# Start addresses in SBUF: weights, xT and the arena on multiples of 2048 bytes, and half the scratch of the software DMA queue

## What is computed

```python
y = (gated_branches(x @ w_in)) @ w_out
x = x + gx1 * y
x = x + gx2 * (square(relu(h @ w_mlp1)) @ w_mlp2)
```

## Time and profile before

| what | value |
|---|---|
| median of 3 runs | 2089.11 us (2085.4 to 2089.83) |
| span of the profiled execution | 2089.1 us, from its first to its last instruction |
| instructions | 36236 |
| TensorE, matmuls | 2024.6 us busy |
| TensorE, weight loads (beside the matmuls) | 1789.9 us busy |
| VectorE | 1363.7 us |
| ScalarE | 1019.1 us |
| GpSimd | 162.3 us |
| granted TensorE clock, mean | 0.991 of full |
| read from HBM | 291.93 MB, 140 GB/s over the span |

### The profile page before, as it was taken

One profiled execution on the slowest core, in us unless ns is written; L12 is line 12 of the kernel. 1 busy time (PEld: TensorE's weight loads), 2 busy tenths in 40 slices (PEclk: granted clock), 3 DMA queues, 4 the chain that ended last, 5 costly groups with the idle time before them and its releaser, 6 DMA issues.

```text
span 2089.1 us, 36236 instructions
## 1 busy us (share of the span) xinstructions
PE 2024.6 (97%) x13946; PEld 1789.9 (86%) x13946; DVE 1363.7 (65%) x2114; ACT 1019.1 (49%) x2014; POOL 162.3 (8%) x174
## 2 busy tenths in 40 slices
PE   6999999999999999999999999999999999999998
PEld 5899657888788888879967999999998989888897
DVE  5699688344565564577977667776766555886455
ACT  5475575324422322358457454445824444675443
POOL 0000000000000001000000002223120111000110
PEclk9999999999999999999999999999999999999999
DMA  7322374222222222233255545554302555443553
GB/s 287 122 82 102 122 283 161 81 101 101 81 83 98 100 100 83 98 108 135 83 203 217 179 147 181 185 192 176 115 21 82 181 181 188 184 164 137 191 183 121
DMA packets 40896, 294.56 MB, mean 141 GB/s; under 512 B 4544, under 2 KB 4544, under 8 KB 5456
## 3 DMA queue, kind: packets, MB, share of 16 engines
q1 hardware_dynamic: 40464, 290.73, 38.4%
q0 software_dynamic: 320, 2.26, 0.3%
HBM read 291.93 MB, written 1.05 MB: 140 GB/s over the span
## 4 chain that ended last, share of the span: by engine, by line
PE 88%; DVE 5%; ACT 4%; issue 1%; DMA 1%; SPq 0%; DVEq 0%; ACTq 0%
PE psum L652 21%; PE psum L654 21%; PE psum L653 20%; PE psum L1017 3%; PE psum L1021 3%; PE psum L1018 3%; PE psum L890 2%; PE psum L1224 2%; DVE weights_lo L1964 2%; PE psum L793 2%; PE psum L912 1%; PE psum L692 1%; PE psum L693 1%; PE psum L694 1%; ACT weights_hi L1363 1%
## 5 line engine op out<-in xcount | busy, mean ns | idle before, releaser
L1964 DVE TENSOR_TENSOR weights_lo<-raw_weights,weights_hi 128x2048 fp32r<-128x2048 f32 x225 | 512.6, 2291 | 163.1 <-ACT weights_hi L1363 162.7
L1363 ACT ACTIVATE weights_hi<-raw_weights 128x2048 fp32r<-128x2048 f32 x225 | 429.0, 1910 | 152.6 <-DMA raw_weights<-in_weights 133.1
L2043 DVE SCALAR_TENSOR_TENSOR xT<-psum,mods,xT 128x256 f32<-128x256 f32 x408 | 181.0, 479 | 199.9 <-PE psum L654 196.5
L652 PE MATMUL psum<-h_hi,weights_hi 128*128 128x512 f32 (+1 forms) x832 | 279.9, 336 | 0.1
L654 PE MATMUL psum<-h_lo,weights_hi 128*128 128x512 f32 (+1 forms) x832 | 279.8, 336 | 0.0
L653 PE MATMUL psum<-h_hi,weights_lo 128*128 128x512 f32 (+1 forms) x832 | 278.1, 334 | 0.0
L2840 POOL TENSOR_TENSOR ffsq<-ff 128x256 f32<-128x256 f32 (+1 forms) x128 | 118.2, 925 | 1592.1 <-ACT ff L1450 1107.6
L652 PE MATMUL psum<-weights_hi,h_hi 128*128 128x256 f32 x704 | 197.5, 280 | 0.0
L653 PE MATMUL psum<-weights_lo,h_hi 128*128 128x256 f32 x704 | 195.5, 278 | 0.0
L654 PE MATMUL psum<-weights_hi,h_lo 128*128 128x256 f32 x704 | 195.5, 278 | 0.0
L652 PE MATMUL psum<-g_hi,weights_hi 128*128 128x256 f32 x688 | 193.7, 282 | 0.0
(11 more groups left out here) (423 smaller groups left out, 4277.6 us busy)
## 6 DMA issues: line engine op xcount, KB each, us to landing
raw_weights<-in_weights SPq DMA_DIRECT2D x273, 1024.0 KB, 4.8
staged_x<-in_x_rows SPq DMA_DIRECT2D x1, 2048.0 KB, 10.0
masks<-in_masks POOLq DMA_DIRECT2D x1, 1152.0 KB, 6.8
ln_rows<-in_ln_rows POOLq DMA_DIRECT2D x1, 1024.0 KB, 6.8
out<-outrow SPq DMA_DIRECT2D x4, 256.0 KB, 2.1
rows<-in_rows SPq DMA_DIRECT2D x1, 584.0 KB, 9.7
consts<-in_consts SPq DMA_DIRECT2D x1, 388.0 KB, 3.8
cols<-in_cols SPq DMA_DIRECT2D x1, 306.0 KB, 2.8
```

The source lines that it names most:

```text
L652: mm(out, *pair(wh, vh), start=i == 0, stop=False)
L1363: f(w_hi[:, s, :], raw[:, s, :], ACT.Copy).then_inc(hi_done, 1)
L1964: tt_(w_lo[:, s, :], raw[:, s, :], w_hi[:, s, :].bitcast(F32), ALU.subtract).then_inc(lo_done, 1)
L2043: last = stt(xT[:, m, c], b[:, c], mods[:, l, which + m, v:v + 1], xT[:, m, c], ALU.mult, ALU.add)
```

## The change

Four edits of constants. The ring of raw weights is moved to address 10240 with a filler tile below it; weights_hi and xT follow it directly and so lie at 43008 and 75776. The arena is rounded up to a multiple of 4096 instead of 64 and lies at 110592. The software queue's scratch is 8192 bytes instead of 16384. The order of the tiles, the offsets within the arena and all instructions are as before. The small tables between xT and the arena move with the ring.

```diff
-        ring_at = -(-nc.sbuf_base // 64) * 64
+        sb("below_ring", [P, (10240 - -(-nc.sbuf_base // 64) * 64) // 4])
+        ring_at = 10240
+        assert nc.sbuf_base == ring_at
         raw = sb("raw_weights", [P, RAW, CHUNK])
...
         ARENA = 112 * 1024
-        arena_at = -(-nc.sbuf_base // 64) * 64
+        arena_at = -(-nc.sbuf_base // 4096) * 4096
...
-    nc = bacc.Bacc("TRN2", target_bir_lowering=False, num_devices=1)
+    nc = bacc.Bacc("TRN2", target_bir_lowering=False, num_devices=1, dynamic_dma_scratch_size=8192)
```

## The result

The changed kernel takes 2096.1 us (median of 6 runs, 2092.97 to 2101.57) against 2088.74 for the kernel before: ratio 1.0037, 95% interval 1.0022 to 1.0052. It is slower, by 7.4 us. (One of the six executions of the kernel before took 5204.07 us; without it their median is 2088.38 and the difference 7.7.) The profiled execution of after spans 2099.8 us, 10.7 more than that of before, and was the longest of its six.

What follows compares the result with a forecast made beforehand. TensorE was taken as the bound (97% busy, 88% of the chain matmuls). From 2089.1 us, TensorE's reads, the splits and the scratch counted 0 and DMA -0.3, giving 2088.8 us; range 2060 to 2104.

Steps and rivals of the forecast that it cites:

- no effect: Likeliest case for the whole kernel: 2088.8 us, own range 2084 to 2093, chance 0.43.
- the case on the slower side: Rival: streamed and loaded operands on equal phase collide, TensorE's level rises; 2109 us in full, 2099 half, chance 0.25.
- TensorE's reads: Term for operand start addresses in matmul triples: taken as 0, between +20 and -24 us.
- that of the rise: Sign of TensorE slowing: pitch over 0.2288 at 700 us or over 0.118 at 150 us.
- that of the fall: Sign of TensorE speeding up (chance 0.32): 0.1133 at 1300 us, or 512 columns under 0.2288 at 700.
- the sign of a wrong reason: Product stretches 550 to 880 and 1250 to 1410 us changing length by over 1 us at equal matmul count.
- The phase modulo 2048 beyond the phase modulo 1024 is worth nothing: Streamed rows at TensorE: crossing a 2048-byte line costs nothing, from even 0.34 us steps and xc_hi's equal booked time.
- An address can't tell those two apart; what came before them can: 256-column stretches at 110 and 150 us: same addresses, different level, so the TensorE term was taken as 0.
- The bounds: Limits on the TensorE term, priced by the trace's two pitch levels: +20 us upward, -24 us downward.
- ScalarE and VectorE, 0: Weight splits (copy 1910 ns, subtraction 2291 ns, 225 times each) unchanged: 0; 1% on both would be 1.9 us.
- DMA, -0.3 us: First transfers' waits at the start, 19.4 us: 3% gain or loss allowed, 0.6 us, half taken.
- The scratch, 0: Halved software-queue scratch for GpSimd's three transfers: cost 0 because covered; 7 us without cover.

Runs made afterwards that it cites:

- x1: Kernel before with only the scratch halved, every tile 8192 bytes lower (ring 8320, arena 106432): 2089.63 us, ratio 1.0002.
- y3: Changed kernel with the arena at 110656, ring still at 10240, restoring the old distances 64 and 192: 2090.94 us, ratio 1.0014.
- x4: Changed kernel with ring (10304) and arena (110656) both 64 bytes past a multiple of 2048, distance 0: 2095.91 us, ratio 1.0042.
- x3: Changed kernel with the ring at 8320, its old phase, and the arena kept at 110592, distance 128: 2112.34 us, ratio 1.0111.
- x2: Changed kernel with the arena at 110528, its old phase, and the ring kept at 10240: 2091.46 us, ratio 1.0010.
- v2: y3 with g, the second network's ff, and h, o and ff of the first network's 256-token layer 128 bytes lower: 2072.14 us, ratio 0.9916.
- z1: x2 with h_hi and h_lo 128 bytes lower: 2090.07 us, ratio 1.0001.
- z2: z1 with ff also at distance 0 for the 512-token MLP and the second network: 2090.25 us, ratio 1.0006.
- v3: v2 with h and ff of the first network's 512-token MLP also at distance 0: 2068.92 us, ratio 0.9896.

## Why the prediction was wrong

The measured 2096.1 us lies inside the range, 2060 to 2104, but the likeliest case was no effect (0.43), and the effect is clear: the case on the slower side, given 0.25, came true in sign, with 7.4 us of its 20. The term that failed is TensorE's reads, put at 0; the product stretches grew by 11.8 us. The signs that were to tell the cases apart came mixed: 0.1200 at 150 us is that of the rise, 0.2266 between 620 and 860 us that of the fall. By these pitches the 1536 matmuls of the first long stretch take some 3 us less and the 1536 of the second some 3 us more, both over the 1 us that was named as the sign of a wrong reason. That the time lies between two of its cases is luck: two effects of opposite sign left a small rest.

- **What bounds the kernel**: right. All of the change lies in TensorE's pitch, none in waits.
- **"The phase modulo 2048 beyond the phase modulo 1024 is worth nothing"**: right, and too weak a test. Steps of 1024 bytes are multiples of 256, so they could not show a period of 256. At 200 us the steps are even in before, x1, y3, after and x4, but not at every distance: in x3 they run from 351 to 362 ns.
- **"An address can't tell those two apart; what came before them can"** is the step that failed. From two levels at one address I took it that addresses set nothing, and the term became 0. The table shows that d sets which pitches are possible. At the distances of the kernel before, 192 and 64, 113.4 and 117.8 ns both are; at d = 0 neither is, and all stretches of over 40 matmuls of 256 columns took 119.6 to 120.0. At 512 columns each d has its pitch to within 1 ns. "Nearest row" was a comparison within one d, which says nothing of another d.
- **The bounds** of +20 and -24 us held, though made of the wrong parts. I bounded each kind by the two levels in the trace; 256 columns went above both (0.1200 against 0.1180) and 512 columns below both (0.2266 against 0.2288). The term for 512 columns had the wrong sign in the rival that came true: it expected +9.7 us from the arena and got -5.4, and the 256-column terms gave +23.5 in place of 9.9.
- **The rival's mechanism**, equal phases that delay each other's reads, fits the 256-column matmuls (x4 shows that equal phases alone bring them) and is contradicted by those of 512, which are at their best with equal phases. A name like "collide" was worth no more than its price.
- **ScalarE and VectorE, 0**: right, 2291 and 1909 ns. **DMA, -0.3 us**: not resolved; the weights land in 4.8 us at either start, so the extra transaction of the Trainium skill, "DMA: Bandwidth & Descriptors", section "How a descriptor splits into AXI transactions", doesn't show in a 1 MB transfer's landing. **The scratch, 0**: right, shown by x1.
- The Trainium skill, "SBUF — State Buffer", section "Who interferes with whom", gives TensorE two read ports, one for the streamed operand and one for the weight load, and calls them independent. The runs differ from that: the pitch moves by up to 3% at 512 columns and 6% at 256 with nothing but the distance of the two operands. That no other engine delays TensorE, which the prediction takes from there, is not tested as such, but the effect needs none: with nothing else at work the pitches move all the same, 229.1 to 226.7 and 117.3 to 120.0 ns.

Open: whether the distance that counts is to the block loaded for the same matmul or to the one being loaded for the next, since in every stretch all loaded blocks had the same d; and what decides between the levels of 256 columns, at d = 192 above all.

## What to carry to other kernels

When TensorE is bound by back-to-back float32r matmuls, measure the pitch of starts by shape and by operand order, and try the distance of the operands' start addresses modulo 256 in steps of 32 or 64 bytes before believing in round addresses; here the distance is worth from -1.0% to over +1%, at no instruction. Compare executions at the same granted clock: here some 5 us of difference came from it. A layout that is best for one matmul shape can be worst for another, so choose it by tile and by stage. Tiles whose stretches alternate did best at one place modulo 256 (second window: x2 and v2 against z1 and z2), though v3 shows that this alone does not hold the lower level. Where the same work shows two speeds at one address, that tells that history matters, not that the address doesn't.

## What was not expected of the hardware

- The pitch of a 256-column matmul with its weight load ranges from 0.1132 to 0.1200 us, that of 512 columns from 0.2266 to 0.2344, as a function of the distance of the two operands' starts modulo 256 bytes, not monotonically: 226.8, 233.2, 228.9, 233.5, 232.4, 234.3, 233.3, 233.3 ns for 512 columns in steps of 32 bytes.
- At distances 192 and 64 a 256-column matmul has two stable pitches, 0.1133 and 0.1178 us. A stretch keeps its level for tens or hundreds of matmuls; at 64 nearly all are high, at 192 g was low in z1 and high in z2, where its neighbour had another distance, and between v2 and v3 the same stretch was at either.
- With no other engine and no transfer at work the distance acts all the same, 229.1 against 226.7 ns for 512 columns and 117.3 against 120.0 for 256.
